# A new order of the early projections, with a few low parts made by GpSimd and a direct sum for the first group

## What is computed

```python
ada = c @ w_ada[l] + b_ada[l]
shift, scale, gate = jnp.split(ada, 3, axis=-1)
h = rms_norm(x, g_pre[l]) * (1.0 + scale[:, None]) + shift[:, None]
proj = h @ w_in[l]          # 2048 x 11328, split into q_mla, c_kv, k_rope, q_diff, k_diff, v_diff, gates
kv = rms_norm(c_kv, g_kv[l]) @ w_ukv[l]
y_mla = (o_mla * jax.nn.silu(gate_mla)) @ w_o_mla[l]
y_diff = (o_diff * jax.nn.silu(gate_diff)) @ w_o_diff[l]
merged = jax.nn.sigmoid(mg_mla) * y_mla + jax.nn.sigmoid(mg_diff) * y_diff
x = x + gate[:, None] * rms_norm(merged @ w_out[l], g_post[l])
```

## Time and profile before

| | |
|---|---|
| median of three runs | 789.84 us (789.74 to 789.95) |
| profiled execution | 788.86 us, span 787.1 us, mean granted clock 0.991 |
| TensorE products | 756.5 us busy, 3533 instructions |
| VectorE | 558.6 us, 812 instructions |
| ScalarE | 399.1 us, 637 instructions |
| GpSimd | 26.2 us, 97 instructions |
| DMA | 189.69 MB, mean 241 GB/s |

### The profile page before, as it was taken

One profiled execution on the slowest core, in us unless ns is written; L12 is line 12 of the kernel. 1 busy time (PEld: TensorE's weight loads), 2 busy tenths in 40 slices (PEclk: granted clock), 3 DMA queues, 4 the chain that ended last, 5 costly groups with the idle time before them and its releaser, 6 DMA issues.

```text
span 787.1 us, 9757 instructions
## 1 busy us (share of the span) xinstructions
PE 756.5 (96%) x3533; PEld 623.1 (79%) x3533; DVE 558.6 (71%) x812; ACT 399.1 (51%) x637; POOL 26.2 (3%) x97
## 2 busy tenths in 40 slices
PE   4689999999999999999999999999999999999995
PEld 4567888878888888888887888888888888888884
DVE  4789998899776878887775777677546546465554
ACT  4456555536566665444454646565444444444441
POOL 3000000000000000000000010111100000000000
PEclk9799999999999999999999999999999999999998
DMA  9999999999665597888874666556666666567642
GB/s 339 388 336 345 357 341 353 311 349 339 206 200 149 192 328 264 286 278 254 287 258 142 207 179 196 166 159 183 177 193 185 171 210 187 185 216 241 219 156 107
DMA packets 117945, 189.69 MB, mean 241 GB/s; under 512 B 10181, under 2 KB 43146, under 8 KB 117642
## 3 DMA queue, kind: packets, MB, share of 16 engines
q1 hardware_dynamic: 117776, 189.04, 74.0%
q10 hardware_dynamic: 122, 0.04, 0.0%
HBM read 185.90 MB, written 2.10 MB: 239 GB/s over the span
## 4 chain that ended last, share of the span: by engine, by line
PE 89%; DVE 5%; issue 2%; SPq 2%; ACT 1%; DMA 1%; POOL 0%; DVEq 0%; POOLq 0%; ACTq 0%
PE ps L1591 27%; PE ps L1595 27%; PE ps L1592 27%; DVE w_both L1329 2%; SPq L428 1%; DVE ada_acc L1126 1%; DMA ada_ring<-in_w_ada 1%; PE ps L1445 1%; PE ps L1421 1%; PE ps L1430 1%; PE ps L1460 1%; PE ps L1434 1%; DVE yg L1353 1%; PE ps L1375 1%; PE ps L1481 1%
## 5 line engine op out<-in xcount | busy, mean ns | idle before, releaser
L1329 DVE TENSOR_TENSOR w_both<-w_raw,w_both 128x1024 fp32r<-128x1024 f32 x248 | 301.2, 1222 | 159.2 <-ACT w_both L884 158.9
L884 ACT CAST w_both<-w_raw 128x1024 fp32r<-128x1024 f32 x248 | 259.3, 1050 | 272.8 <-PE ps L1595 214.5
L1591 PE MATMUL ps<-w_both,h_hi 128*128 128x512 f32 x704 | 282.5, 401 | 5.4 <-DVE w_both L1329 5.2
L1595 PE MATMUL ps<-w_both,h_lo 128*128 128x512 f32 x704 | 275.6, 392 | 0.7 <-DVE h_lo L1229 0.7
L1592 PE MATMUL ps<-w_both,h_hi 128*128 128x512 f32 x704 | 274.9, 391 | 0.0
L1591 PEld LDWEIGHTS ps<-w_both,h_hi 128*128 128x128 f32 x704 | 132.7, 188 | 38.3 <-issue 9.4
L1595 PEld LDWEIGHTS ps<-w_both,h_lo 128*128 128x128 f32 x704 | 132.5, 188 | 29.5 <-DVE h_lo L1229 1.1
L1592 PEld LDWEIGHTS ps<-w_both,h_hi 128*128 128x128 f32 x704 | 132.7, 188 | 27.2 <-issue 1.0
L1126 DVE SCALAR_TENSOR_TENSOR ada_acc<-ada_ring,cols,ada_acc 128x512 f32<-128x512 f32 x112 | 78.4, 746 | 1.8 <-DMA ada_ring<-in_w_ada 1.8
L1591 PE MATMUL ps<-w_both,o_hi 128*128 128x512 f32 x128 | 50.6, 395 | 0.0
L1126 DVE SCALAR_TENSOR_TENSOR ada_acc<-gate_ring,cols,ada_acc 128x512 f32<-128x512 f32 x60 | 44.8, 747 | 7.6 <-DMA gate_ring<-in_w_ada 6.7
(11 more groups left out here) (223 smaller groups left out, 611.2 us busy)
## 6 DMA issues: line engine op xcount, KB each, us to landing
w_raw<-in_w_in SPq DMA_DIRECT2D x177, 512.0 KB, 4.7
ada_ring<-in_w_ada SPq DMA_DIRECT2D x128, 256.0 KB, 6.3
gate_ring<-in_w_ada SPq DMA_DIRECT2D x32, 512.0 KB, 4.4
w_raw<-in_w_out SPq DMA_DIRECT2D x32, 512.0 KB, 3.7
w_raw<-in_w_o_mla SPq DMA_DIRECT2D x16, 512.0 KB, 3.6
w_raw<-in_w_o_diff SPq DMA_DIRECT2D x16, 512.0 KB, 4.4
w_raw<-in_w_ukv SPq DMA_DIRECT2D x8, 512.0 KB, 4.5
x_tok<-in_x SPq DMA_DIRECT2D x2, 1024.0 KB, 6.1
```

Source lines behind the costliest of these rows:

```text
L884: act.copy(w_hi[:, p % RING, :], w_raw[:, p % RING, :]).then_inc(hi_done, 1)
L1329: dve.tensor_tensor(w_lo[:, p % RING, :], w_raw[:, p % RING, :], w_hi[:, p % RING, :].bitcast(F32), ALU.subtract).then_inc(lo_done, 1)
L1591: mm(o, lhsT=s_hi[:, k, q], rhs=hi, start=first and r == 0, stop=False)
L1595: ins = mm(o, lhsT=s_lo[:, k, q], rhs=hi, start=False, stop=last and r == tiles - 1)
```

## The change

- **Plan.** Only q0 and q1 remain running sums (banks 0 to 3); q2 becomes a projection of visits, with its part sum in q_part. Visits alternate between banks 4, 5 and 6, 7 (early_bank), so a visit waits for the one before the last; a turn uses the bank of the visit that would come next. The first three periods have eight pieces each (6, 7 and 8 before), the next have 9, 10, 10, 10 and 7: 70 pieces in phase 1, 28 visits, 20 of them added by VectorE. The turns stand in front of pieces 6, 14, 21, 29, 40, 50 and 60 (5, 12, 20, 30, 40, 50 and 60 before). The work on ada rows is spread from one turn to the next, and comes behind the piece's load and low part rather than ahead of them. The number of pieces in the whole kernel is the same.
- **Start.** Piece 0 is loaded behind all eight ada loads of group 0. VectorE sums 13 of the 16 rows of group 0; TensorE takes rows (5, 0), (5, 1) and (7, 1) directly as products with one column, and sums the two accumulators over partitions in the same way, so the transposes, the join and ScalarE's sums of this group go. VectorE reads the four columns and makes mod_shift and mod_gain (first_mod); ScalarE and VectorE make h_hi and h_lo tile by tile. ScalarE copies all eight groups of xT.
- **Order in a piece.** In the first piece that uses a new pair of h, all products with h_hi come first, those with h_lo last.
- **GpSimd** makes the low part of 18 pieces (2, 3, 5, 10, 12, 14, 18, 20, 22, 26, 28, 30, 35, 38, 45, 48, 55, 58), each a 128x1024 subtraction with both inputs in SBUF.
- **Joining.** In the other groups the halves are joined ahead of the last two rows, which then go into one accumulator.
- **Smaller.** The angles are computed in four parts at four pieces; ScalarE sums a turned group one piece earlier than it makes h; at the end the sum of the first three squares is made ahead, GpSimd adds the fourth itself, and the last output part is split in two.

```diff
+TURN = "turn"
 PERIODS = [
-    [(("vd", 0), (0,)), 0, (("vd", 1), (0,)), 1, (("gate", 0), (0,)), 2],
-    [(("gate", 1), (0, 1)), 0, (("gate", 2), (0, 1)), 1, 2],
-    [(("gate", 3), (0, 1, 2)), 0, (("vd", 0), (1, 2)), 1, 2],
-    [(("ckv", 0), (0, 1, 2, 3)), 0, (("vd", 1), (1, 2, 3)), 1, 2],
-    [(("gate", 0), (1, 2, 3, 4)), 0, (("gate", 1), (2, 3, 4)), 1, 2],
-    [(("gate", 2), (2, 3, 4, 5)), 0, (("gate", 3), (3, 4, 5)), 1, 2],
-    [(("vd", 0), (3, 4, 5, 6)), 0, (("vd", 1), (4, 5, 6)), 1, 2],
-    [(("ckv", 0), (4, 5, 6, 7)), 0, (("gate", 0), (5, 6, 7)), 1, 2],
+    [(("vd", 0), (0,)), (("vd", 1), (0,)), 0, (("gate", 0), (0,)), (("gate", 1), (0,)), (("gate", 2), (0,)), TURN, 1,
+     (("q", 2), (0,))],
+    [(("ckv", 0), (0, 1)), 0, (("gate", 3), (0, 1)), (("vd", 0), (1,)), TURN, 1, (("vd", 1), (1,))],
+    [(("gate", 0), (1, 2)), 0, (("gate", 1), (1, 2)), TURN, 1, (("gate", 2), (1, 2))],
+    [(("vd", 0), (2, 3)), 0, (("vd", 1), (2, 3)), TURN, 1, (("q", 2), (1, 2, 3))],
+    [(("ckv", 0), (2, 3, 4)), 0, (("gate", 3), (2, 3, 4)), TURN, 1, (("gate", 0), (3, 4))],
+    [(("gate", 1), (3, 4, 5)), 0, (("gate", 2), (3, 4, 5)), TURN, 1, (("vd", 0), (4, 5))],
+    [(("vd", 1), (4, 5, 6)), 0, (("q", 2), (4, 5, 6)), TURN, 1, (("gate", 0), (5, 6))],
+    [(("ckv", 0), (5, 6, 7)), 0, (("q", 2), (7,)), 1, (("gate", 0), (7,))],
...
+OPENING = [v for v, visit in enumerate(VISITS) if visit[1] not in [w[1] for w in VISITS[:v]]]
+ADDING = [v for v in range(len(VISITS)) if v not in OPENING]
+LAST_VISIT = {visit[1]: v for v, visit in enumerate(VISITS)}
...
+FIRST_ON_PE = {(5, 0), (5, 1), (7, 1)}
+POOL_PART = [(2, 3, 5)] + [(2, 4, 6)] * 3 + [(2, 5)] * 3 + [()]
+OUT_PARTS = [(t, slice(c, c + CH)) for t in range(TOK) for c in range(0, D, CH)]
+OUT_PARTS[-1:] = [(TOK - 1, slice(c, c + CH // 2)) for c in (D - CH, D - CH // 2)]
...
+            if step == TURN:
+                sum_before[len(pieces)] = j + 1
...
+    POOL_LO = [first_part[j][i] for j in range(KT // 2) for i in POOL_PART[j]]
...
-        return 6 if a is None else 2 * a if a < 3 else 2 * ((a + 1) % 2)
+        return 2 * (a % 2)
+
+    def early_bank(v):
+
+        return 4 + 2 * (v % 2)
...
+        turn_at = {j: place for place, j in sum_before.items()}
+        ada_after = {}
+        for j in range(1, KT // 2):
+            begin = turn_at.get(j - 1, 0)
             for q in range(KT // 2):
-                place = 1 + q // 2 if j == 0 else q * (len(own) - 1) // (KT // 2)
-                ada_before.setdefault(own[place], []).append((j + 1, q))
-
-
-        sum_before = {first_part[j][-1]: j + 1 for j in range(KT // 2 - 1)}
-        sums_until = lambda p: 1 + sum(place <= p for place in sum_before)
-        h_after = {0: 0} | {place + 2: j for place, j in sum_before.items()}
+                place = min(q, turn_at[1] - 1) if j == 1 else begin + q * (turn_at[j] - begin) // (KT // 2)
+                ada_after.setdefault(place, []).append((j, q))
+
+
+        h_after = {place + 2: j for place, j in sum_before.items()}
+        h_lo_before = {place + 3: j for place, j in sum_before.items()}
...
             for q in range(KT // 2):
-                if q == KT // 2 - 2:
-                    load_piece(0, *pieces[0][1:4])
                 load_ada(0, q)
+            load_piece(0, *pieces[0][1:4])
             for p, (a, kind, n, i, first, last) in enumerate(pieces):
-                for j, q in ada_before.get(p, ()):
-                    load_ada(j, q)
                 if p >= 1:
                     load_piece(p, kind, n, i)
+                for j, q in ada_after.get(p, ()):
+                    load_ada(j, q)
                 if p == 40:
                     with nc.allow_non_contiguous_dma(reason="256 positions, once"):
                         sp.dma_start(pos_q[:, :], positions[0, :].rearrange("(t p) -> p t", p=P)).then_inc(pos_in, 16)
...
+            for p in POOL_LO:
+                pool.wait_ge(hi_done, p + 1)
+                nc.gpsimd.tensor_tensor(w_lo[:, p % RING, :], w_raw[:, p % RING, :], w_hi[:, p % RING, :].bitcast(F32),
+                                        ALU.subtract).then_inc(lo_pool, 1)
...
-                pool.wait_ge(y_sums, t + 1)
-                nc.gpsimd.tensor_scalar(variance[:, R_Y, t:t + 1], sumsq[:, R_Y, t:t + 1], 1.0 / D, EPS,
+                pool.wait_ge(y_sums, 1)
+                pool.wait_ge(y_squared[t], 4)
+                nc.gpsimd.tensor_scalar(variance[:, R_Y, t:t + 1], y_sq[:, t, 3:4], 1.0 / D, sumsq[:, R_Y, t:t + 1],
...
+            def make_first_h():
+
+                eng.wait_ge(xT_copied, KT // 2)
+                eng.wait_ge(mod_first, 1)
+                for k in range(2):
+                    act.activation(h_hi[:, k, :], xnT[:, k, :], ACT.Identity, scale=mod_gain[:, k:k + 1],
+                                   bias=mod_shift[:, k:k + 1]).then_inc(h_first_hi, 1)
...
+            def first_rows(q):
+
+                eng.wait_ge(ada_in[q], 32)
+                for t, done, count, amount in ((1, ada_odd, q - (q > 5), 3 if q == 6 else 1),
+                                               (0, ada_used, q - (q == 6), 2 if q == 6 else 1)):
+                    if (q, t) in FIRST_ON_PE:
+                        continue
+                    row = ada_slot(q)[:, t, :, :].rearrange("p s n -> p (s n)")
+                    cc = cols[:, V_C + 2 * q + t:V_C + 2 * q + t + 1]
+                    if q == 0:
+                        ins = dve.tensor_scalar(ada_acc[:, t, :], row, cc, None, ALU.mult)
+                    else:
+                        eng.wait_ge(done, count)
+                        ins = dve.scalar_tensor_tensor(out=ada_acc[:, t, :], in0=row, scalar=cc, in1=ada_acc[:, t, :],
+                                                       op0=ALU.mult, op1=ALU.add)
+                    ins.then_inc(done, amount)
+
+            def first_mod():
+
+                eng.wait_ge(ada_turned, 1)
+                dve.tensor_tensor(mod_shift[:, 0:2], ps[:, 2, 0:2], cols[:, V_SHIFT:V_SHIFT + 2], ALU.add)
+                link(eng, dve.tensor_tensor(mod_gain[:, 0:2], ps[:, 2, 2:4], cols[:, V_GPRE:V_GPRE + 2], ALU.mult))
+                dve.tensor_tensor(mod_gain[:, 0:2], mod_gain[:, 0:2], cols[:, V_SCALE:V_SCALE + 2],
+                                  ALU.add).then_inc(mod_first, 1)
+
+            def make_first_h_lo():
+
+                eng.wait_ge(mod_first, 1)
+                eng.wait_ge(xT_copied, KT // 2)
+                full = [stage[:, 0, k * SEQ:(k + 1) * SEQ] for k in range(2)]
+                for k in range(2):
+                    dve.tensor_scalar(full[k], xnT[:, k, :], mod_gain[:, k:k + 1], mod_shift[:, k:k + 1], ALU.mult,
+                                      ALU.add).then_inc(h_first_full, 1)
+                for k in range(2):
+                    eng.wait_ge(h_first_full, k + 1)
+                    eng.wait_ge(h_first_hi, k + 1)
...
+                if p not in POOL_LO:
+                    eng.wait_ge(hi_done, p + 1)
                 if kind == "kr":
                     dve.tensor_tensor(kr_half(p, 1), kr_raw_piece(p), kr_half(p, 0).bitcast(F32),
                                       ALU.subtract).then_inc(lo_done, 1)
-                else:
+                elif p not in POOL_LO:
                     dve.tensor_tensor(w_lo[:, p % RING, :], w_raw[:, p % RING, :],
                                       w_hi[:, p % RING, :].bitcast(F32), ALU.subtract).then_inc(lo_done, 1)
                 for r in rows[1:]:
                     gate_row(r)(eng)
-                if p in h_after:
-                    make_h_lo(h_after[p])
-                if p == PH1 - 6:
-                    angles()
+                if p == 0:
+                    first_mod()
+                    make_first_h_lo()
+                for j, q in ada_after.get(p, ()):
+                    ada_part(j, q)
...
-                pe.wait_ge(ada_joined, j + 1)
-                if j:
-                    pe.wait_ge(ada_read, j)
-                    visits = sum(end < place for end in visit_end for place, k in sum_before.items() if k == j)
-                    if visits:
-                        pe.wait_ge(early_read, visits)
+                pe.wait_ge(ada_used, (j + 1) * (KT // 2))
+                if j >= 2:
+                    pe.wait_ge(ada_read, j - 1)
+                if turn_visits(j) >= 2:
+                    wait_visit(pe, turn_visits(j) - 2)
...
+            def first_sum(src, cc, first):
+
+                for b in range(4):
+                    ins = mm(ps[:, 2, b:b + 1], lhsT=src(b), rhs=cc, start=first and b == 0, stop=False,
+                             skip_group_check=True)
+                return ins
+
+            def first_direct(q, first):
+
+                pe.wait_ge(ada_in[q], 32)
+                for t in range(2):
+                    if (q, t) in FIRST_ON_PE:
+                        ins = first_sum(lambda b: ada_slot(q)[:, t, b // 2, b % 2 * P:(b % 2 + 1) * P],
```

(62 more changed lines are left out.)

217 lines of the change are left out of this document (109 added, 108 removed).

## The result

The change made the kernel slower: 795.16 us, median of four runs (794.86 to 796.32), against 789.79 (789.23 to 789.95) on the same chip, a ratio of 1.0076 with a 95% interval of 1.0063 to 1.0090. The forecast was 779.9; 795.16 also lies just outside its range of 776.5 to 794. The profiled execution took 795.15 us, with a span of 793.4 (before: 787.1).

A forecast was written before the change was run, and what follows sets the result against it. TensorE was taken as the bound, busy without a break from 63 us, so gains lay before that and in the tail: 788.86 - 8.8 - 1.1 = 778.96, plus 0.98 for the median, 779.9 us; range 776.5 to 794.

The forecast's parts named there:

- Start: Opening, up to the first product: it would start at 24.8 us (24.3 to 26), 5.0 us earlier.
- Phase 1 without GpSimd: Stretch up to the eighth turn, GpSimd's subtraction costing VectorE 0: turn at 196.6 us, 8.8 us earlier.
- The steps in between: Additions to 60 pieces of 2.796 us on TensorE: slow clock 1.5, DMA 1.5, VectorE's tightest stretch 1.0 us.
- The room of 28 us: VectorE's slack up to the eighth turn: its work ends at 168.1 us, against 196 for TensorE.
- rival 1: Phase 1: GpSimd's subtraction holds VectorE for its whole length; eighth turn 208.3, time 791.7 us (788 to 797), chance 0.35.
- What GpSimd's subtraction costs: Phase 1: VectorE time lost to each GpSimd low part, bounds 0 and 2.2 us, taken as 0.
- Tail: Behind the last product: first output product at 780.7 instead of 781.99; 1.1 us gained (0.5 to 1.4).
- Rivals 2 and 3: One: each subtraction costs VectorE 1.1 us, 784.9 us, chance 0.14; other: DMA keeps 358 GB/s, 784 us, chance 0.08.
- A part price: Phase 1: each GpSimd subtraction costs VectorE the 1.1 us it spares; time 784.9 us, chance 0.14.
- Rival 3's sign: Phase 1: ScalarE's casts waiting for w_raw up to 90 us would show DMA keeping 358 GB/s; chance 0.08.

## Why the prediction was wrong

**Start: right in this execution, with luck.** 24.8 forecast, 24.25 measured; piece 0's low part ended at 23.08 for 23.4, and no low h of piece 0 held TensorE. But of the nine profiled executions with the new start (one of them with piece 0 loaded earlier) four had their first product at 27.2 to 27.5, beyond the 24.3 to 26 of the forecast, which had no term for it.

**Phase 1 without GpSimd: close.** TensorE, DMA and VectorE together were to bring the eighth turn to 196.6. Without GpSimd's part it came at 198.35, in spite of 18 more low parts on VectorE. The steps in between cost 5.9 us over 60 x 2.796, where I had allowed 4.0. Of what I took for VectorE (145.9, or 166.2 with those 18) the run shows 170.6 busy: 4.4 too little, 2.3 of it for two low parts that it makes ahead of the turn. The room of 28 us that rival 1 had to use up was thus smaller: 22.2 + 170.6 - 20.3 = 172.5 against 196.6 leaves 24, and the price from which it decides is 1.3 us a piece, not 1.55. Even that counts on VectorE using all of its idle time, which it did in neither kernel with GpSimd's part.

**"What GpSimd's subtraction costs": the step that failed.** I had bounds of 0 and 2.2 us for what one piece takes from VectorE and took 0; it was 1.9. The whole miss of the direction is in it: 13.4 us of time between the changed kernel and the one without this part, against a forecast gain of 9.9. The row I chose by the earlier trace rows was VectorE's subtraction of 1.23 us started inside a GpSimd power of 0.69. It was no accident: five low parts of the kernel before started inside such a power, all of 1.22 or 1.23 us. But that power handles two columns, and so was no test of an operation that reads 1024. Why it holds nothing no run shows; shown is that a copy with 1024 columns holds VectorE and fills do not. The row beside it, the product that waited to VectorE's very end, showed the mechanism for GpSimd's side, and I had no row of like size that spoke against it for VectorE's: it should have carried the sum.

**Rival 1 was right in mechanism and low by 3.5 us.** It put the eighth turn at 208.3, and it came at 211.97. Its terms, with what was measured: VectorE's own work 4.4 more than assumed; the lock 34.6 in place of 43.2 - 3 = 40.2, so 5.6 less (GpSimd's piece was longer than its 2.2 us, 2.39 alone and 2.78 here, but part of the 2.78 is GpSimd's own waiting for the VectorE operation in front of it, and a held operation lost at most 2.2); and 4.5 us (189.8 - 185.28) in which VectorE was idle, for which the rival had nothing. 208.3 + 4.4 - 5.6 + 4.5 = 211.6. Of those idle microseconds 3.1 stand before low parts, waiting for casts, and 1.5 before low h. TensorE's lower clock after the 3.55 us wait shows in its busy time; since VectorE set the pace there, I don't add it as a term of its own.

**Tail: half of it.** Forecast 1.1. From the last square's read to the first output product it was 2.50 and is 1.38 (below): 1.1, as worked out. But from that product to the end of the span it is 5.7 us and was 5.1, so 0.5 is left. Of the 0.6 that went, the split product costs 2.87 - 2.74 = 0.13; the rest lies between the last product and the end of the span (2.85 us for 2.37), where I had allowed the smaller transfer a gain of 0.1. That stretch was 2.51 in the run with the new end alone, so it differs between executions by 0.3. The tail of the changed kernel:

```profile
786.30 0.19 ACT L803 ACTIVATION_READ_ACCUMULATOR act_junk<-ps 128x1 f32 x1
787.68 2.87 DVE L1458 SCALAR_TENSOR_TENSOR yg<-yg,rstd,x_again 128x512 f32<-128x512 f32 x5 [0.46 <-POOL rstd L625]
```

**Rivals 2 and 3: not seen.** A part price of 1.1 us a piece was too low. DMA did fall under 358 GB/s, but as a consequence: without GpSimd's part it moved 393 GB/s up to 60 us and 394 from 60 to 80. Rival 3's sign was there even so: ScalarE's casts waited for w_raw 16 times up to 100 us, 17.9 us in all; TensorE's waits for low parts up to the eighth turn then came to only 1.9.

The best version is the change without GpSimd's part: 781.8 us, 0.9% under the kernel before and 1.7% under the changed one. It is 1.9 above the forecast, which had counted on GpSimd's help at no price.

## What to carry to other kernels

Before giving elementwise work to GpSimd, count what VectorE runs beside it: if those operations have two inputs in SBUF, each GpSimd operation that reads as many columns can hold one of them almost for its own duration (here up to 2.2 of 2.39 us), to be set against the VectorE time spared (here 1.9 lost for 1.1 spared). Idle time of VectorE is no cover by itself: at 89% busy, waiting at the same places as before, it paid in full, while in the last 56 pieces, where the two engines seldom met, it paid nothing. A short neighbour that runs undisturbed is no evidence for a long one: look at how many columns each reads, and take a row that shows a lock in one direction as showing it in both until a row of like size speaks against it. And sum an engine's busy time with the relief at both prices: here it was at 97% up to the eighth turn without the relief, and 14.6 us more of work became 13.7 us of time.
